# The order of the first microseconds of a hybrid attention layer: warm-up matmuls divided around the first transposes, and VectorE's first steps reordered

## The reference

```
h   = RMSNorm_pre(x)                      # x * rsqrt(mean(x*x) + eps) * g
u   = h @ W_in                            # 8 groups of 512 columns
A   = differential attention (two softmax maps, learned lambda, per-head norm)
B   = block-sparse attention (top-k past blocks and the own causal block)
y   = concat(A * silu(gate_a), B * silu(gate_b)) @ W_out
out = x + RMSNorm_post(y)
```

## Time and profile before

| | us |
|---|---|
| median of three executions | 254.51 |
| lowest and highest | 254.19 and 254.54 |
| the profiled execution | 254.41 |
| its span, first to last instruction | 252.5 |

### The profile page before, as it was taken

The page is one execution under the profiler, slowest core; times in us unless marked ns, Lnnn a source line. Parts: engine busy times, 40 slices in busy tenths (PEclk is TensorE's granted clock), DMA queues, the critical chain, the costliest instruction groups (busy, mean ns, idle before and its releaser), DMA issues.

```text
span 252.5 us, 4454 instructions
## 1 busy us (share of the span) xinstructions
PE 245.4 (97%) x1569; PEld 123.1 (49%) x1569; DVE 176.8 (70%) x393; ACT 142.8 (57%) x336; POOL 32.2 (13%) x74
## 2 busy tenths in 40 slices
PE   7999999999999999999999999999999999999991
PEld 7444444445454554544455444454444454555570
DVE  2898586487468688868877767977787896835313
ACT  4677566165356667574677595667565665611110
POOL 2129300000000320041032033000000000111101
PEclk9999999999999999999999999999999999999998
DMA  7968989605555544544935654679849769982422
GB/s 241 401 203 189 310 269 378 207 6 135 106 163 159 180 114 128 148 155 115 209 96 134 139 159 120 129 186 170 169 130 220 192 158 167 203 202 43 125 86 83
DMA packets 59674, 42.47 MB, mean 168 GB/s; under 512 B 45808, under 2 KB 46072, under 8 KB 59652
## 3 DMA queue, kind: packets, MB, share of 16 engines
q1 hardware_dynamic: 59636, 42.18, 63.9%
q10 hardware_dynamic: 16, 0.00, 0.0%
HBM read 29.04 MB, written 2.13 MB: 123 GB/s over the span
## 4 chain that ended last, share of the span: by engine, by line
PE 93%; DMA 3%; SPq 1%; DVE 0%; DVEq 0%; issue 0%; POOLq 0%; ACT 0%; POOL 0%; ACTq 0%
PE unit_ps L574 72%; PE score_ps L630 6%; PE o_ps L651 5%; PE unit_ps L604 4%; DMA stage<-in_w_in_dram 3%; PE unit_ps L611 2%; PE unit_ps L585 1%; PE score_ps L703 1%; PE unit_ps L703 1%; SPq L364 0%; PE score_ps L532 0%; SPq L395 0%; DVE area L1052 0%; DVEq L180 0%; POOLq L180 0%
## 5 line engine op out<-in xcount | busy, mean ns | idle before, releaser
L574 PE MATMUL unit_ps<-area,w_hi 128*128 128x512 f16 x256 | 76.2, 379 | 0.0
L782 ACT ACTIVATE arena<-arena,negmax 128x512 f32<-128x512 f32 (+3 forms) x64 | 35.4, 554 | 49.6 <-DVE negmax L979 49.4
L574 PE MATMUL unit_ps<-w_hi,area 128*128 128x512 f16 x192 | 60.3, 379 | 0.0
L574 PE MATMUL unit_ps<-area,w_lo 128*128 128x512 f16 x128 | 48.5, 379 | 0.0
L574 PEld LDWEIGHTS unit_ps<-area,w_hi 128*128 128x128 f16 x256 | 24.1, 98 | 27.2 <-issue 1.1
L574 PE MATMUL unit_ps<-w_lo,area 128*128 128x512 f16 x96 | 36.4, 379 | 0.0
L979 DVE CUSTOM_DVE_ANT_0 arena<-score_ps,strips 128x512 f32<-128x512 f32 (+3 forms) x64 | 28.6, 483 | 9.3 <-PE score_ps L630 9.3
L876 DVE SCALAR_TENSOR_TENSOR w_lo<-stage,g_cols,w_hi 128x512 f16<-128x512 f32 x32 | 24.1, 754 | 10.4 <-ACT w_hi L740 10.3
L574 PEld LDWEIGHTS unit_ps<-w_hi,area 128*128 128x128 f16 x192 | 18.8, 98 | 21.9 <-DVE w_lo L882 0.7
L739 ACT ACTIVATE w_hi<-stage,g_cols 128x512 f16<-128x512 f32 x32 | 22.7, 710 | 6.6 <-DMA stage<-in_w_in_dram 6.4
L878 DVE SCALAR_TENSOR_TENSOR w_lo<-stage,g_cols,w_hi 128x512 f16<-128x512 f32 x32 | 24.8, 776 | 0.0
(11 more groups left out here) (106 smaller groups left out, 356.4 us busy)
## 6 DMA issues: line engine op xcount, KB each, us to landing
stage<-in_w_in_dram SPq DMA_DIRECT2D x32, 512.0 KB, 4.1
stage<-in_w_out_dram SPq DMA_DIRECT2D x8, 512.0 KB, 4.3
arena<-in_x_dram SPq DMA_DIRECT2D x4, 512.0 KB, 8.7
strips<-bias_rows SPq DMA_DIRECT2D x4, 512.0 KB, 4.4
stage<-in_x_dram SPq DMA_DIRECT2D x4, 512.0 KB, 4.4
out_dram<-area SPq DMA_DIRECT2D x3, 512.0 KB, 2.8
strips<-bias_rows SPq DMA_DIRECT2D x1, 1024.0 KB, 7.0
pt<-arena SPq DMA_TRANSPOSE x32, 3.1
```

Of the source, the lines that this page charges most:

```text
L574: last = nc.tensor.matmul(bank, a, b, start=(k == 0 and n == 0), stop=(k == KT - 1 and n == 2))
L782: nc.scalar.activation(probs[:, i % 2, m, 0:n], probs[:, i % 2, m, 0:n], ACT.Exp, bias=negmax[:, i, m:m + 1], scale=-1.0, accum_out=sums[: ...
```

## The change

The eight warm-up matmuls become 4, 1 and 3: four ahead of g's transpose, one between it and the wait for x's tile 0, and three between the transposes of tile 0 and `first_quarter(0)`. DVE reads g's columns first, then sums the squares, and weights the first four blocks before it adds the two sums of squares. Nothing else is changed, and both kernels do the same work.

```diff
-    WARM_UP = 8
+    WARM_UP = [4, 1, 3]
...
             pe.wait_ge(warm_ready, 1)
-            warm_up(WARM_UP)
+            warm_up(WARM_UP[0])
             pe.wait_ge(consts_ready, 2)
             pe.wait_ge(gpre_loaded, 16)
             nc.tensor.transpose(unit_ps[:, 0, 0:KT], g_rows[:, :], ident[0:KT, 0:KT]).then_inc(g_turned, 1)
+            warm_up(WARM_UP[1])
             pe.wait_ge(x_loaded[0], 16)
             for part in range(2):
                 x_transposes(0, range(part * KT // 2, (part + 1) * KT // 2), x_first_turned)
+            warm_up(WARM_UP[2])
             for q in range(4):
                 first_quarter(q)
...
             nc.vector.memset(warm, 1.0).then_inc(warm_ready, 1)
-            x_half_square(0)
-            x_mean_square(0)
             dve.wait_ge(g_turned, 1)
             nc.vector.tensor_scalar(g_cols[:, :], unit_ps[:, 0, 0:KT], W_SCALE, 1.0, ALU.mult,
                                     ALU.mult).then_inc(g_scaled, 1)
+            x_half_square(0)
             dve.wait_ge(g_scaled, 1)
             x_weigh(0)
+            x_mean_square(0)
             x_weigh(1)
             x_norm(0)
             split(0)
```

## The result

| kernel | executions | median us | lowest to highest |
|---|---|---|---|
| before | 18 | 254.5 | 253.88 to 255.88 |
| changed | 18 | 255.14 | 254.54 to 257.09 |

The ratio is 1.0035, with a 95% interval of 1.002 to 1.0051. The change makes the kernel 0.6 us slower; 254.5 with no difference was forecast. The time lies just inside the range of 253.9 to 255.2, which is no merit of the mechanism: the case that I held likeliest was 254.2 to 254.8. Three of the 18 are over 256.4, against none before.

The account below looks back on a forecast made before the run. PE was taken to bound the kernel, its gapless run starting at quarter 2's landing. Warm-up, DVE and DMA at 0 and PE at most -0.1, from 254.41 profiled (median 254.51), gave 254.5, range 253.9 to 255.2.

Parts of the forecast that it names:

- the case that I held likeliest: Change works but is hidden behind the landings of quarter 2 and tile 2, clock up in time: chance 0.62.
- What bounds the kernel: PE never waits from 11.02 us to its last matmul; quarter 2's landing sets that start, so at most 0.1 gained.
- DVE's reordering at nothing: g's columns fill DVE's idle time before 3.99 us; other DVE work hides the later addition of squares: 0 us.
- Quarter 4's issue at nothing: The load of W's quarter 4 is issued about 0.4 us earlier, off the chain: 0 taken.
- The clock: Step on PE's clock at the start: rise read at about 4.4 us after 3.4 us of matmuls without a gap.
- the cover ahead of quarter 2: PE's idle time before quarter 2 lands at 10.88 us, expected to swallow most of a 1.6 us loss.
- rises late, by one step: Rival, chance 0.13: clock rises at 7.4 to 7.9 us because the warm-up is broken; 254.8 to 255.0.
- later still: Rival, chance 0.14: clock rises at 9.2 us or beyond, as transposes may not count; 255.7, or 256.7.
- What follows: PE after tile 0: `first_quarter(0)` at 5.7 us, `first_quarter(1)` done by 10.1; 0.6 us won becomes idle before quarter 2.
- The gaps: PE idle gaps of 0.7 us behind the clock's rise, as at 10.1 to 11.0, should cost nothing.
- The transposes: Whether PE transposes count as work for the clock's release; the skill says not, the earlier trace does not show it.
- the case at 9.2: Clock rise at 9.2 us if transposes do not count: `first_quarter(0)` ends at 9.9, ordinary units 1.2 us later, 255.7.

Follow-up runs that it names:

- 4, 1, 3 with the old order: Changed kernel's warm-up division, but VectorE's order as in the kernel before: 254.77 us, ratio 1.0007; its profiled execution took 256.0.
- 4, 1, 0: Changed kernel without the three warm-up matmuls behind tile 0's transposes: 255.43 us, ratio 1.0024.
- 4, 4, 3: Changed kernel with three more warm-up matmuls between g's transpose and the wait for x's tile 0: 255.16 us, ratio 1.0025.
- 8, 0, 3: Changed kernel with eight warm-up matmuls ahead of g's transpose, none behind it, three behind tile 0's transposes: 254.44 and 254.89 us in two runs.
- the clock raised beforehand: Both kernels with 40 warm-up matmuls in front, loads held back: before 266.26, changed 266.13 us; loads released by the 28th: 264.35 and 263.98.
- 5, 2, 0: Changed kernel with five warm-up matmuls ahead of g's transpose, two behind it, none behind tile 0's transposes: 254.57 us, ratio 1.0004.
- 8, 0, 0: Changed kernel with all eight warm-up matmuls in front again, VectorE's new order kept: 254.52 and 254.59 us in two runs.

## Why the prediction was wrong

**What bounds the kernel: right for the change.** PE has no wait behind the start of the ordinary units. In the profiles of before, of the changed kernel, of 4, 1, 3 with the old order, of no warm-up and of 4, 1, 0, the span is the start of those units plus 236.9 us: 15.57 and 252.5, 16.04 and 252.9, 17.30 and 254.2, 16.87 and 253.8, 17.01 and 253.9. In the other profiles it is 237.3 in 4, 4, 3 and 237.4 to 237.5 in the two of 8, 0, 3, and 236.9 to 237.2 in the rest. So up to 0.6 us can come behind the start, as much as the effect itself. In 4, 4, 3 0.3 us of it is a wait of PE for a small transfer (`pt<-arena`); in 8, 0, 3 PE has no such wait, and the cause is open.

**DVE's reordering at nothing: right with eight in front** (0.9997 for the new order alone), and no wait for DVE stands in the changed kernel's profile behind tile 0. Quarter 4's issue at nothing: no chain shown here runs through it.

**"The clock": this is the step that failed.** I read one rise, at 4.4 after an unbroken warm-up, and gave 0.62 to the clock being up in time, with the transposes at 0.87 us and the three matmuls at 0.65. The changed kernel's profile has 1.97 and 0.99: 1.44 us lost at 1.2 GHz, of which the cover ahead of quarter 2 hid about half; 0.47 us were left at the ordinary units. The rise is at about 7.0 there and at about 7.6 and 9.8 in the other two profiles with 4, 1, 3. Even with the unbroken eight it came at 4.4 in one profile and at about 5.9 to 7.0 in the four others. The rival "rises late, by one step" is what the changed kernel's profile shows, and its price, 0.3 to 0.5, was about right, in part by luck: the rise came earlier than its 7.4, and tile 0 landed 0.43 us later than I had it. The rival "later still" is seen once, in the profile of 256.0 with the old order; the executions of the changed kernel from 255.8 to 257.1 may be of this kind, but none of them was profiled. To the two together I gave 0.27, and all three profiles of 4, 1, 3 belong to them.

**"What follows": the cover was a draw, and smaller than it looked.** Tile 0 was first used between 3.98 and 4.44 us in the profiles whose loads start with the kernel, quarter 2 between 9.82 and 11.38, and tile 2 between 12.47 and 14.56. Where PE is late, or the transfers early, PE is the chain from tile 0 on, and what is put on its list between 4 and 11 us shows in the time. The three matmuls behind the transposes, costed at nothing, are then on the path: 0.99 us in the changed kernel's first profile, 1.28 in its second and in the one with the old order. What they cost net is not settled: about 0.25 us at the high clock by two profiles and 0.26 in the median with eight in front, which by itself is not clear of the spread, and taking them out of 4, 1, 3 won nothing (255.43).

**The gaps: open.** I held gaps of 0.7 us behind the rise harmless from the end of the kernel, where the clock is granted for 3.2 us after the last matmul. Idle pieces of 1.45 and 0.71 us, and one of 1.03 us, left the clock up in two profiles with the clock raised beforehand; 0.66 and 1.27 us, shortly after each other, were followed by its halving in a third.

**The transposes:** I had left open if they count for the clock. They do.

Two smaller things: four warm-up matmuls were to end at 2.8 us, and g's transpose began at 3.26 in the changed kernel's profile, which cost nothing; and the "same four pieces" of the case at 9.2 are five, as its own list says.

Why a divided or shorter warm-up leaves the clock low for longer is open: the unequal rises of equal kernels say that something outside PE's list takes part. That the low clock is the near cause of the loss is shown by the profiles, where 1.44 us are lost to it ahead of quarter 2, and by the steps in the times from no warm-up to eight (0.8 us) and from 4, 1, 0 to 5, 2, 0 (0.9 us). The missing loss with the clock held up fits but rests on too few executions, and late landings of tile 2 lengthen executions beside it.

## What to carry to other kernels

A warm-up ahead of a critical start should last, without idle time, until the data lands: 5, 2, 0 did as well as 8, 0, 0, and 4, 1, 0 did not. A dummy matmul behind the data's landing is work on the path whenever no transfer covers it, and at the low clock it takes twice as long. Slack read from one execution, against a transfer or against the rise of the clock, is a draw; before costing something at nothing by it, ask by how much the landing moves between executions, and who is the chain when it is early.

## What I had not expected of the hardware

- The rise of PE's clock under the same 3.8 us of float32 matmuls from 1.04 us came at 4.4 in one execution and at about 5.9 to 7.0 in four others; with seven of them in one piece from 1.62 it came at about 7.8. The column of the granted clock reads 1.00 in both stretches; only the pace (421 ns in the median of the warm-up's records, 1.97 against 0.87 us for eight transposes) shows the low level.
- The landing of the same load of 0.5 MB, seventh in its queue, moved by up to 2 us between executions (first used at 12.47 in one, landed at 14.54 in another) in kernels whose loads up to there are identical.
- Transposes alone can raise the clock: it was up after 13 float32 ones in 3.0 us.
